# Filter tiles one step sooner, and the context spectra ahead of the latent ones, in the input projection of the even layer

## The reference, cut to what matters

```python
u_ctx = h_ctx @ w_in
u_lat = h_lat @ w_in
...
h = jnp.sin(freq * (z @ w1 + b1))
h = jnp.sin(freq * (h @ w2 + b2))
h = (h @ w3).reshape(L, HY_ORDER, D_HY)
h = h * window[:, None, :]
...
y = irfft(rfft(z, n=2 * L) * rfft(h, n=2 * L))[:, L // 2: L // 2 + L]
```

## Time and profile before

| What | us |
|---|---|
| median of three runs (lowest, highest) | 3385.66 (3383.9, 3386.74) |
| the profiled execution, its own time | 3384.87 |
| its span, first to last instruction | 3383.2 |
| TensorE busy in the span | 3162.0 (93%) |
| VectorE busy | 1836.0 (54%) |
| ScalarE busy | 914.9 (27%) |
| GpSimd busy | 419.3 (12%) |

### The profile page before, as it was taken

One profiled execution on the slowest core, in us unless ns is written; L12 is line 12 of the kernel. 1 busy time (PEld: TensorE's weight loads), 2 busy tenths in 40 slices (PEclk: granted clock), 3 DMA queues, 4 the chain that ended last, 5 costly groups with the idle time before them and its releaser, 6 DMA issues. The chain is left out here.

```text
span 3383.2 us, 38060 instructions
## 1 busy us (share of the span) xinstructions
PE 3162.0 (93%) x14722; PEld 2521.9 (75%) x14722; DVE 1836.0 (54%) x2660; ACT 914.9 (27%) x1049; POOL 419.3 (12%) x391
## 2 busy tenths in 40 slices
PE   7999987999766999999999999899969999999999
PEld 6777854555554888888888888787858888888887
DVE  5666556576687354444554455677773433333333
ACT  4211133444112131111111111477772211111111
POOL 1000000777421200000000011200001000000000
PEclk8999998999888999999999999999989999999999
DMA  5454400003113112222222222211112111111111
GB/s 193 155 176 151 136 2 1 1 1 121 53 49 143 44 41 75 75 74 74 74 74 81 80 85 68 81 37 40 37 69 77 50 50 50 50 43 50 44 55 75
DMA packets 73131, 240.01 MB, mean 71 GB/s; under 512 B 9703, under 2 KB 19303, under 8 KB 71496
## 3 DMA queue, kind: packets, MB, share of 16 engines
q1 hardware_dynamic: 48296, 174.09, 14.8%
q0 software_dynamic: 14240, 50.94, 4.6%
q10 hardware_dynamic: 10496, 13.63, 1.2%
HBM read 212.94 MB, written 25.69 MB: 71 GB/s over the span
## 5 line engine op out<-in xcount | busy, mean ns | idle before, releaser
L254 PE MATMUL bank<-h_pair,w_hi 128*128 128x512 f32 (+1 forms) x2448 | 620.1, 380 | 8.1 <-DVE h_pair L1894 7.2
L254 PEld LDWEIGHTS bank<-h_pair,w_hi 128*128 128x128 f32 x2448 | 442.3, 188 | 97.3 <-issue 8.9
L240 DVE TENSOR_TENSOR w_lo<-w_raw,w_hi 128x1024 fp32r<-128x1024 f32 x194 | 263.9, 1360 | 369.3 <-ACT w_hi L234 366.1
L270 PE MATMUL bank<-h_pair,w_hi 128*128 128x512 f32 x1344 | 366.8, 394 | 0.0
L234 ACT ACTIVATE w_hi<-w_raw 128x1024 fp32r<-128x1024 f32 x194 | 203.9, 1051 | 555.2 <-PE bank L270 218.4
L254 PE MATMUL bank<-h_pair,w_lo 128*128 128x512 f32 (+1 forms) x1224 | 353.4, 379 | 0.0
L1825 DVE SCALAR_TENSOR_TENSOR x<-bank,c_mods,x 128x1024 f32<-128x1024 f32 (+3 forms) x280 | 273.8, 1006 | 144.2 <-PE bank L254 141.1
L270 PEld LDWEIGHTS bank<-h_pair,w_hi 128*128 128x128 f32 x1344 | 228.0, 188 | 43.4
L254 PEld LDWEIGHTS bank<-h_pair,w_lo 128*128 128x128 f32 x1224 | 221.2, 188 | 44.0
L270 PE MATMUL bank<-h_pair,w_lo 128*128 128x512 f32 x672 | 208.3, 391 | 0.0
L270 PE MATMUL bank<-hid_pair,w_hi 128*128 128x512 f32 x704 | 192.9, 395 | 0.0
(11 more groups left out here) (367 smaller groups left out, 5200.2 us busy)
## 6 DMA issues: line engine op xcount, KB each, us to landing
w_raw<-in_weights SPq DMA_DIRECT2D x194, 512.0 KB, 3.2
ada_rows<-in_ada_rows POOLq DMA_DIRECT2D x86, 256.0 KB, 3.7
ada_early<-in_ada_early SPq DMA_DIRECT2D x48, 256.0 KB, 3.0
c_rows<-in_ada_rows POOLq DMA_DIRECT2D x42, 256.0 KB, 3.6
x<-in_x SPq DMA_DIRECT2D x2, 5120.0 KB, 15.3
h_gate<-u_scratch SPq DMA_DIRECT2D x4, 2560.0 KB, 9.9
ada_w<-in_ada_w SPq DMA_DIRECT2D x16, 512.0 KB, 16.9
u_scratch<-uc POOLq DMA_DIRECT2D x12, 640.0 KB, 3.5
```

Of the source, the lines that this page charges most:

```text
L240: e.tensor_tensor(k.w_lo[s][:, :], k.w[s][:, :], k.w_hi[s][:, :].bitcast(F32), ALU.subtract).then_inc(k.split_lo[s], 1)
L254: mm = e.matmul(out[:, c:c + m], w[:, c1:c1 + P], x[:, c:c + m], start=(first and kk == 0 and n == 0), stop=(last and kk == kt - 1 and n = ...
L270: mm = e.matmul(out[:, c:c + m], w, x[:, half, c:c + m], start=(first and n == 0), stop=(last and n == 2))
```

## The change

It has three parts. In `even_in_events` the tiles 4 and 5 of a pass stand behind steps 3 and 4 of item b + 1 where they stood behind steps 4 and 5. In `POS` the two context spectra come first, so that they are g = 0 and 1 and the latent ones g = 2 to 8. In `butterflies` the context part comes first and signals `xh_ready` by itself, and the latent part signals again behind it; so the counter rises by two in a pass, and whoever waits for it waits for twice the count. Every spectrum now waits for the count that its own part needs.

```diff
-        at = [(b, kk) for kk in range(4, KT)] + [(b + 1, kk) for kk in (4, 5)]
+        at = [(b, kk) for kk in range(4, KT)] + [(b + 1, kk) for kk in (3, 4)]
...
-    POS = [("lat", pos, r) for pos, r in enumerate(ORDER_LAT)] + [("ctx", pos, r) for pos, r in enumerate(ORDER_CTX)]
+    POS = [("ctx", pos, r) for pos, r in enumerate(ORDER_CTX)] + [("lat", pos, r) for pos, r in enumerate(ORDER_LAT)]
...
-                    e.wait_ge(xh_ready, i // 3)
+                    e.wait_ge(xh_ready, 2 * (i // 3))
...
                     e.wait_ge(hw_ready, NM * (p + 1))
-                    e.wait_ge(xh_ready, p + 1)
                 else:
                     e.wait_ge(spec_read, NP * p + g)
                 part, pos, r = POS[g]
+                e.wait_ge(xh_ready, 2 * p + (1 if part == "ctx" else 2))
...
-                        e.wait_ge(xh_ready, len(FILTER_PASSES))
+                        e.wait_ge(xh_ready, 2 * len(FILTER_PASSES))
...
+                butterfly_ctx(e, steps, hw[:, M_LAT:NT], xh_ctx)
+                steps.settle()
+                e.sem_inc(xh_ready, 1)
                 butterfly_lat(e, steps, hw[:, 0:M_LAT], xh, spec[:, 0:10])
-                butterfly_ctx(e, steps, hw[:, M_LAT:NT], xh_ctx)
                 e.sem_inc(xh_ready, 1)
```

## The result

The changed kernel takes 3363.68 us in the median of four runs (3363.17 to 3365.01), against 3385.61 us (3383.9 to 3386.74) for the kernel before in the same session: a ratio of 0.9939 with an interval of 0.9927 to 0.9950. That is 21.9 us less; the forecast was 3359.0 with a range of 3354 to 3366, 26.5 us less. The profiled execution took 3363.25 us, with a span of 3361.6.

The account below looks back on a forecast made before the run. TensorE bounds the projection, waiting four times for VectorE's butterflies (16.3 us) and then slowed by the clock. Four gaps, 6.62 us each: 3384.87 - 26.5 = 3358.4, plus 0.8 for the timed median, 3359.2; forecast 3359, range 3354 to 3366.

Parts of the forecast that it names:

- rival (a): Projection's four gaps: only idleness returns fully, clock's share smaller in timed runs; up to 9.5 us less gain; chance 0.07.
- The four gaps and their removal: Input projection: TensorE waits four times for the butterflies' signal, then runs at 1.2 GHz; removal gains 6.62 us each, 26.5 together.
- The order carries the gain, the tiles widen the margin: Projection: context first alone has 1.9 us to spare; earlier tiles alone leave 2.5 us of idleness.
- The margins of 3.5 and 1.9 us: Third spectrum of a pass: latent signal comes 3.5 us early with both parts, 1.9 us with the order alone.
- The covers: Slack formerly shadowed by the gap: VectorE idle 9.60 to about 3.3 us, GpSimd's loads 4 us left; none used up.
- The added waits: 32 spectra on TensorE get a wait for `xh_ready`, all satisfied beforehand: taken as 0, upper end 1.6 us.
- (b): Third spectrum of each pass: the wait moves there as latent butterflies end late; 3363, at worst 3385.7 us; chance 0.05.
- (c): Tile 0 of passes 1 to 3: GpSimd's loads come late; at 15 us longer landing, 3392 us; chance 0.02.
- What TensorE gains in these items moves everything after it forward: From the projection to the kernel's end: nothing hides the gain, so the full 26.5 us reach the end.
- the term of zero for the stretch behind: Phases behind the projection: the sum contains no gain or loss there.
- rival (d): Stages behind the projection: gaps there may lose less to the clock; some 5 us more gain, 3354 or below; chance 0.04.
- its last sentence: Sign: if the projection gains 26.5 us and the end does not, the difference was given back in the phases behind.

Follow-up runs that it names:

- the filled gap: Kernel before with 18 spare matmuls on TensorE ahead of the wait for the butterflies' signal in each pass: 3375.38 us (0.9977).
- the cut kernels: Kernels before, after and with spare matmuls in the gaps, each ended behind the input projection: 447.41, 419.56 and 437.83 us.
- the other session's ratio: Kernel after once more, unchanged, against the kernel before in that session: 3364.91 us (0.9941).
- the ten executions of the table: Profiled executions: three of before, two of after, one each of tiles only, order only, gap filled, 5 and 13 spare matmuls; clock fall and Hyena piece read, no joint time.
- the one shift that was to bring the time back: Kernel after with 13 spare matmuls between items 14 and 15: 3366.32 us (0.9950).
- the one with the stalls: Kernel after with 34 spare matmuls ahead of the last transposes of the latents phase and 14 behind them: 3372.78 us (0.9967).

## Why the prediction was right, and where its sum was off

The direction held, and so did the mechanism in the projection itself. That the whole kernel's time lies in the range is in part luck: 3363.7 is what the prediction had for rival (a) (3364 in the middle), which did not come; the missing us were lost behind the projection, and for a loss there its range had no room of its own above the forecast. Point by point:

- **The four gaps and their removal.** 17.0 us of idleness and 9.5 us of clock were predicted; the filled gap measured 16.9 and 9.4 us one by one, the profiles of before and after 26.4 together, the cut kernels 27.9 in timed runs, about 1 of it in the start.
- **The order carries the gain, the tiles widen the margin.** Shown by the two single parts: 0.9940 for the order, as for both, and 2.3 us of wait left in each pass for the tiles alone. The margins of 3.5 and 1.9 us were read as 3.5 and 1.7.
- **The covers.** VectorE's idle time went from 9.60 to 2.23 us, about a us lower than the 3.3 predicted: item 4 has 18 instead of 20 pairs of spectra matmuls, which the prediction says, but it did not move the item's end by those 0.88 us; GpSimd's loads kept 5.9 us. Neither was used up. The added waits on TensorE cost nothing that can be read: the distances of 2.62 and 3.47 us are those without them.
- **The rivals.** (b) and (c) did not come, and (a) did not either: the gaps of 4.2 us lost the same in all three profiled executions of before. At (a) the prediction named the rule of the Trainium skill ("TensorE: Matmul & The Clock Gate", Part 1), that the moment of the clock's change is not tied to the kernel and shifts from run to run. For these gaps it would have made the loss vary, and the profiles don't agree. They agree with it elsewhere: in the tiles-only kernel the same wait of 2.3 us cost clock in two passes and none in two.
- **The step that was off** is the sentence "What TensorE gains in these items moves everything after it forward", and with it the term of zero for the stretch behind. It measured +3.3 us in the first pair of profiles and +3.1 to +5.5 between any other profile of before and of after. The prediction named such a change only as rival (d), as a gain, with 0.04, though its last sentence names the sign of such a difference: the stretch gains 26.5 us and the end does not. With this term the sum is 26.4 - 3.3 = 23.1 us, if the start takes as long in both; 21.9 were measured (20.0 by the other session's ratio, 0.9941).

What stays open is why the stretch behind is longer after the change. Shown is that it has the same instructions, that the extra time of the first pair of profiles lies in a part of the Hyena phase with a lower granted clock, and that this part takes 88.3 or 91.7 us whatever order and signals the projection has. Kernels with the same code behind range from 2949.7 to 2959.0 us. That the moment of the gaps against the clock's changes decides is argued, from the ten executions of the table, and not shown: the one shift that was to bring the time back did not move the phases against the clock.

## What to carry to other kernels

A wait on the busiest engine has two prices, its own length and the slower clock behind it; here the second was more than half of the first, and filling the wait with unused matmuls separates the two. When a consumer needs only a part of what a producer signals at once, put the small part first and give it a signal of its own: it costs no work, and it was worth all of the gain here. And do not carry a gain in one stage to the end one for one where the stages behind have gaps: allow some us of clock for them. Where a number rests on a single stage, compare that stage between like points of several profiles; its length repeated to 0.6 us here, while the timed runs of one kernel spread over 8 us (3379.88 to 3388.09).

## What the runs showed of the hardware that I had not expected

- A wait of TensorE of 2.3 us brought the granted clock of the next 5 to 6 us down to 0.70 in two passes and left it at 1.00 in two others of the same execution.
- The same 12658 matmul records behind the projection took 2949.7 to 2959.0 us of span, over kernels that differ only ahead of them (leaving out the one with the stalls).
- Unused matmuls in a wait held the clock through the wait but not through the short waits behind them (1.00, then 0.55).
- TensorE stood still for 1.04 and 2.21 us with nothing that the profile shows to wait for, far behind an edit that had added 48 matmuls to its program; another kernel with 72 more had no such stall.
- The first 96 us were granted 0.84 of the clock in some executions and 0.82 in others, over the same code, and item 2 started at 96.5 to 97.5 us in the ones and at 97.6 to 98.2 in the others.
